# Attention stage: length rows as split products, the gate unit ahead of each step's scores, four output units in the last steps

## The chip, the cores and the metric

The kernel runs on one core of one Trainium2 chip, as one launch. The metric is the device time of that launch in microseconds (us), median of the runs. The engines are TensorE (PE in the rows, its weight loads PEld), VectorE (DVE), ScalarE (ACT), GpSimd (POOL) and SyncE (SP), which issues the weight loads of the kernel from DRAM. Each engine works through its own list of instructions; semaphores tie the lists together.

## The reference, cut to what matters

The model is two blocks of two layers each on 256 tokens of width 1024. The first block's layer is a feed-forward part, a token mixer and a second feed-forward part. The token mixer has a gated delta rule branch (y_a) and an attention branch (y_b):

```python
def mla(...):
    q = (rms_norm(q_lat, q_lat_gain) @ w_q_up).reshape(B, S, MLA_HEADS, MLA_QK)
    kv = (rms_norm(kv_lat, kv_lat_gain) @ w_kv_up).reshape(B, S, MLA_HEADS, QK_NOPE + V_HEAD)
    ...
    q = rms_norm(q, q_norm)
    k = rms_norm(k, k_norm)
    ...
    o = causal_block_attention(q, k, v)

def token_mix(...):
    y_a = gated_deltanet(...) @ w_branch_a
    y_b = mla(...) @ w_branch_b
    y = jax.nn.sigmoid(gate_a) * y_a + jax.nn.sigmoid(gate_b) * y_b
    return y @ w_out
```

gated_deltanet ends with an rms_norm of each head's output, times a gate. The change touches only the two token mixers of the first block (two layers).

## The kernel before

Everything lies transposed: 128 channels on the partitions, T = 256 tokens along the free axis, so a 1024-wide activation is 8 tiles of 128 x 256. All large products are float32 made of three rounded products (three_pass, L589 to L591): weights and activations are each split into a rounded part (hi) and the rest (lo), and hi x hi, lo x hi and hi x lo are added in PSUM. A **unit** is 128 x 1024 weights, 24 such matmuls of 128 x 256. SP streams the units in the order of use into a ring of 8 slots (raw), a slot being free once the unit 8 before it is done (unit_done). ScalarE rounds a unit to w_hi (split_hi, L544), VectorE subtracts to get w_lo (split_lo, L557; lo_ready), both 4 units ahead of TensorE (AHEAD).

Stages follow each other with their instructions written out by hand for each engine. In each of the two layers three stages matter here:

- **up** (up_tensor and so on): queries, keys and values from the latents. In between, the delta rule's heads get their lengths: o_sums adds squares, o_inverse and a Sqrt give rinv (16 rows, one per head), o_length (L1609) spreads row h over 128 partitions by a product of a column of the identity with rinv, in float32 with 16 rows. At its end the first two gate units (gate_a, m = 0, 1) run; the length rows of the attention heads (rinv16, named soft in the rows) are made from up_summed by a reciprocal and a Sqrt (L1782); L1755 turns them to columns.
- **attn** (attn_tensor and so on): 8 heads, one per step i. TensorE: length row of head i+2 (L1855), scores of head i (L1873, L1874; float32), gate unit i+2 (while i+2 < 8), then the turn of the weights of head i-3 (L1885, three transposes) and the product of head i-4 (L1893, L1894). VectorE: mask and maximum (L1922), nmx (L1926), keys of head i+2 (L1905, L1906), split_lo, the scaling of head i-1. ScalarE: Exp of head i (L1953), split_hi, the Tanh of gate unit i+1 (gate_a_scalar, L1846), the copy of the turned weights (pt, L1964) and of the product (qn, L1968). After step 5 there are no gate units left, and steps 6 to 11 hold scores, turns and products alone.
- **gates** (gates_tensor and so on): 24 units, gate_b (g), the output product of the delta rule branch (a) and of the attention branch (b), in the order GATE_UNITS; first both branch outputs are rounded and subtracted (o_hi L2014, o_lo L2042; 2048 columns each), then 8 units of w_out.

PSUM has 8 banks. The gate units use GATE_A_BANKS = (0, 1, 5, 7, 5, 7, 5, 7), so from m = 4 on a unit waits until the Tanh of unit m-2 has read its bank:

```python
    if m >= 4:
        pe.wait_ge(p.sem["gate_act"], attn.at("gate_act") + m - 1)
```

len_parts and pick_r are in use before the change too, in the projection stage: 64 rows of rounded parts and 64 of rests, of which pick_r takes one of each, so one rounded product of 128 rows spreads a length row (L1028).

Of the kernel before, what the change touches and what calls it, by code (L numbers as in the profile page):

```python
# [13 lines left out]
P = 128  # L14
T = 256
# [268 lines left out]
def signals(st):  # L284
# [15 lines left out]
    if kind == "gdn":  # L300
        n = dict(gdn_step=2 * PAIRS, cols_ready=1, exp_cum=1, rows_done=8,
                 kb_ready=8, exponent_ready=16, row_exp=8, decay_ready=8, pairs_done=8, pairs_used=16, sq_done=8,
                 inv_grown=2 * GROWN, turned_done=8, turned_used=8, first_turned=2 * PAIRS, conv_pad=1,
                 first_both=4 * PAIRS, lp_done=2 * MERGES, lq_done=2 * MERGES, new_ready=2 * MERGES, wu_done=8,
                 v0_ready=8, state_done=8, state_ready=8, v1_done=8, v1_ready=8, o_done=8,
                 out_ready=8, sums_done=1, inv_step=1, o_inv=1, o_sq=8, o_root=1, len_row=8, o_gated=8, oa_ready=8)
    if kind == "up":
        n = dict(lat_sq=6, up_out=20, up_summed=20, up_sq=20, lat_sum=1, lat_ready=5, lat_var=2,
                 lat_root=1, lat_rows=2, lat_scaled=5, lat_rounded=5, rope_in=5, rope_out=5, rope_step=10, rope_turned=5,
                 rinv_rows=1, values_out=4, head_var=3, cols_done=1, cols_ready=2)  # L310
    if kind == "attn":
# [41 lines left out]
class Program:  # L353


    def __init__(self, nc, ctx, stages, dram):
# [68 lines left out]
        self.qn = self.over("qn", 39936, [P, HEADS, T])  # L425
        self.qr = self.over("qr", 48128, [P, HEADS // 2, T])
        self.vt = self.over("vt", 52224, [P, 2, D])
        self.krz = self.over("krz", 60416, [P, HEADS, T])
        self.kr = self.over("kr", 68608, [P, T])
        self.work = self.over("work", 69632, [P, 2, T])  # L430
        self.rinv16 = self.soft
        self.sm = self.over("sm", 8192, [P, ATTN_AHEAD + 1, 3 * P])
        self.o_lo = self.over("o_lo", 8192, [P, 16, T], F32R)
        self.o_hi = self.over("o_hi", 48128, [P, 16, T], F32R)
# [1325 lines left out]
def up_scalar(p, act, st):  # L1760
    a, u0, nc, f = st.at, st.unit0, p.nc, p.nc.scalar.activation
    for j in range(N_UP):
        if j < 12:
            if j % 2 == 0:
                split_hi(p, act, u0 + AHEAD + j // 2)
            if j == 4:
                act.wait_ge(p.sem["o_inv"], st.gdn.at("o_inv") + 1)
                f(p.rinv[0:16], p.rinv[0:16], ACT.Sqrt).then_inc(p.sem["o_root"], 1)
        elif j % 4 == 0:
            split_hi(p, act, u0 + AHEAD + 6 + (j - 12) // 4)  # L1770
            act.wait_ge(p.sem["o_gated"], st.gdn.at("o_gated") + HEADS)
# [10 lines left out]
    f(p.rinv16[0:16], p.rinv16[0:16], ACT.Sqrt).then_inc(p.sem["rinv_rows"], 1)  # L1782


def up_vector(p, dve, st):
# [18 lines left out]
    for j in range(5):  # L1804
        out = p.kr[:] if j == 4 else p.qr[:, j]
# [5 lines left out]
    for s in range(8, 10):  # L1811
        split_lo(p, dve, u0 + AHEAD + s)

    dve.wait_ge(p.sem["up_summed"], a("up_summed") + N_UP)
    v.tensor_scalar(p.rinv16[0:16], p.psum[0:16, 6, 0:T], 1.0 / 192, EPS, ALU.mult, ALU.add).then_inc(
        p.sem["head_var"], 1)
    dve.wait_ge(p.sem["head_var"], a("head_var") + 2)
    v.reciprocal(p.rinv16[0:16], p.rinv16[0:16]).then_inc(p.sem["head_var"], 1)
# [29 lines left out]

def attn_tensor(p, pe, st):
# [3 lines left out]
    def length(h):  # L1853

        mm(p.psum[:, 2 + h % 2, 0:T], p.c("ident")[0:16, HEADS + h : HEADS + h + 1].to_broadcast([16, P]),  # L1855
           p.rinv16[0:16], start=True, stop=True).then_inc(p.sem["head_rinv"], 1)

    pe.wait_ge(p.sem["values_out"], a("values_out"))
    for h in range(2):
        length(h)  # L1860
    for i in range(HEADS + ATTN_AHEAD + 1):
        if i < HEADS:
# [13 lines left out]
        if i + 2 < KD:  # L1876
            gate_a(p, pe, st, i + 2)
# [20 lines left out]
def attn_vector(p, dve, st):  # L1898
# [15 lines left out]
    for i in range(HEADS + 1):  # L1914
# [16 lines left out]
        if i:  # L1931
# [7 lines left out]
                p.sem["weighed"], 1)  # L1939


def attn_scalar(p, act, st):
# [4 lines left out]
    for i in range(HEADS + ATTN_AHEAD + 1):  # L1947
        if i < HEADS:
# [29 lines left out]
def gates_tensor(p, pe, st):  # L1978
    a, u0 = st.at, st.unit0
    pe.wait_ge(p.sem["ob_out"], a("ob_out"))  # L1980
    freed = []
    for n, (kind, m) in enumerate(GATE_UNITS):
        if n >= 4:
            sem, count = freed[n - 4]
            pe.wait_ge(p.sem[sem], count)
        freed.append(("gate_act", a("gate_act") + m + 1) if kind == "g" else ("y_step", a("y_step") + 2 * m + (1 if kind == "a" else 2)))
        pe.wait_ge(p.sem["lo_ready"], u0 + n + 1)
        if kind != "g" and m == 0:
            pe.wait_ge(p.sem["o_split"], a("o_split") + (1 if kind == "a" else 2))
        hi, lo, first = dict(g=(p.h_hi, p.h_lo, 0), a=(p.o_hi, p.o_lo, 0), b=(p.o_hi, p.o_lo, 8))[kind]  # L1990
        for k in range(UNIT):
            ins = three_pass(p, p.psum[:, n % 4, 0:T], (u0 + n) % SLOTS, k, hi[:, first + k], lo[:, first + k],
# [15 lines left out]
def gates_scalar(p, act, st):  # L2008
# [28 lines left out]
def gates_vector(p, dve, st):  # L2037
    a, u0, v, x = st.at, st.unit0, p.nc.vector, st.x(p)
    for b, src in enumerate((p.qkv[:, 0:HEADS], p.qn[:])):
        dve.wait_ge(p.sem["o_rounded"], a("o_rounded") + b + 1)  # L2040
        part = slice(8 * b, 8 * b + 8)
        v.tensor_tensor(p.o_lo[:, part], src, p.o_hi[:, part].bitcast(F32), ALU.subtract).then_inc(p.sem["o_split"], 1)  # L2042
# [694 lines left out]
def plan():  # L2737
# [47 lines left out]
    for at, st in enumerate(stages):  # L2785
# [131 lines left out]
```

## Time and profile before

| | us |
|---|---|
| median of 3 runs | 3016.95 (3011.16 to 3019.12) |
| the profiled execution's own time | 3017.49 |
| its span in the profile | 3015.7 |
| TensorE busy | 2863.1 (95%) |
| VectorE busy | 2266.2 (75%) |
| ScalarE busy | 1405.8 (47%) |

The granted clock of TensorE is given in the window views as PEclk, where 1.00 is 2.4 GHz and 0.50 is 1.2 GHz; over the run its mean is 0.973. The attention stage of the first layer lies at 502 to 555 us, that of the second at 1301 to 1354. In the timeline a row's second number is the time from its start to its modelled end, and matmuls overlap, so the time that a piece of work takes on TensorE is read from start to start.

### The profile page before, as it was taken

Reading aid. Unit: us, or ns where it says so; the run is one execution under the profiler, and the core shown is the slowest. Engines: PE = TensorE matmul, PEld = TensorE weight load, DVE = VectorE, ACT = ScalarE, POOL = GpSimd, SP = SyncE. Lnnn points to the kernel's source line nnn. Section 1 sums busy time; section 2 is a strip of 40 time slices with the busy share of each in tenths; the row PEclk is TensorE's granted clock in tenths of the full one; section 3 lists DMA queues with packets and bytes.
Section 4 is the critical chain, followed back from the end, with each engine's and each line's share of the span. In section 5 each row is a group of like instructions: output and inputs, shape, how many; then the busy total and the mean of one; then the engine's idle time right before and its main releaser. Section 6 shows DMA issues by size and latency. Waiting matters only on the chain.

```text
span 3015.7 us, 61676 instructions
## 1 busy us (share of the span) xinstructions
PE 2863.1 (95%) x24692; PEld 2753.7 (91%) x24692; DVE 2266.2 (75%) x3616; ACT 1405.8 (47%) x2286; POOL 414.9 (14%) x444
## 2 busy tenths in 40 slices
PE   5999999999999999999999999899999999998998
PEld 5999887899999988779999999799987999998998
DVE  7999665578877786556787888788887688777554
ACT  3436533444444464444444446544676444443342
POOL 0025001010200210200102012201036101002001
PEclk9999999999999999999999999999999899999899
DMA  8995302358967642125787885388421488675353
GB/s 339 355 367 181 126 9 99 132 190 332 333 232 281 220 166 71 57 71 189 255 309 265 309 322 170 122 316 324 169 99 64 164 310 328 226 264 187 119 188 127
DMA packets 172726, 632.21 MB, mean 210 GB/s; under 512 B 19168, under 2 KB 19552, under 8 KB 172000
## 3 DMA queue, kind: packets, MB, share of 16 engines
q1 hardware_dynamic: 123696, 450.79, 41.6%
q10 hardware_dynamic: 48816, 178.41, 16.6%
q8 instruction: 154, 2.52, 0.3%
q14 instruction: 60, 0.49, 0.1%
HBM read 628.07 MB, written 1.05 MB: 209 GB/s over the span
## 4 chain that ended last, share of the span: by engine, by line
PE 86%; DVE 9%; ACT 3%; issue 1%; DMA 1%; POOL 0%; DVEq 0%; ACTq 0%; POOLq 0%
PE psum L589 24%; PE psum L590 23%; PE psum L591 23%; DVE w_lo L557 3%; PE psum L607 1%; PE psum L608 1%; DVE ada_w L636 1%; DVE xl L2315 1%; PE psum L613 1%; PE psum L2411 1%; PE psum L1523 1%; PE psum L1526 1%; ACT w_hi L544 1%; PE psum L2431 1%; PE psum L2425 1%
## 5 line engine op out<-in xcount | busy, mean ns | idle before, releaser
L589 PE MATMUL psum<-h_hi,w_hi 128*128 128x256 f32 x4464 | 1256.3, 281 | 0.9 <-ACT qn L1968 0.9
L590 PE MATMUL psum<-h_hi,w_lo 128*128 128x256 f32 x4464 | 1250.6, 280 | 0.0
L591 PE MATMUL psum<-h_lo,w_hi 128*128 128x256 f32 x4464 | 1248.5, 280 | 0.0
L557 DVE TENSOR_TENSOR w_lo<-raw,w_hi 128x1024 fp32r<-128x1024 f32 x852 | 1065.9, 1253 | 180.1 <-ACT w_hi L544 179.2
L544 ACT ACTIVATE w_hi<-raw 128x1024 fp32r<-128x1024 f32 x852 | 875.6, 1055 | 386.9 <-DMA raw<-stream_dram 232.8
L589 PEld LDWEIGHTS psum<-h_hi,w_hi 128*128 128x128 f32 x4464 | 843.0, 189 | 3.7 <-ACT qn L1968 1.3
L590 PEld LDWEIGHTS psum<-h_hi,w_lo 128*128 128x128 f32 x4464 | 842.9, 189 | 0.7 <-issue 0.2
L591 PEld LDWEIGHTS psum<-h_lo,w_hi 128*128 128x128 f32 x4464 | 842.7, 189 | 0.0
L590 PE MATMUL psum<-u_hi,w_lo 128*128 128x256 f32 x1584 | 442.7, 279 | 0.0
L589 PE MATMUL psum<-u_hi,w_hi 128*128 128x256 f32 x1584 | 442.5, 279 | 0.0
L591 PE MATMUL psum<-u_lo,w_hi 128*128 128x256 f32 x1584 | 441.9, 279 | 0.0
L636 DVE CUSTOM_DVE_ANT_0 ada_w<-ada_w,tmp 128x1024 f32<-128x1024 f32 x312 | 386.0, 1250 | 3.4 <-ACT tmp L644 3.4
L901 ACT ACTIVATE gate<-psum 128x256 f32<-128x256 f32 x198 | 76.1, 384 | 587.1 <-PE psum L591 573.6
L730 POOL TENSOR_TENSOR tmp<-x 128x256 f32<-128x256 f32 x91 | 112.3, 1237 | 1629.7 <-DVE x L951 1235.0
L591 PEld LDWEIGHTS psum<-u_lo,w_hi 128*128 128x128 f32 x1584 | 297.8, 188 | 0.0
L590 PEld LDWEIGHTS psum<-u_hi,w_lo 128*128 128x128 f32 x1584 | 297.7, 188 | 0.0
L589 PEld LDWEIGHTS psum<-u_hi,w_hi 128*128 128x128 f32 x1584 | 297.7, 188 | 0.0
L928 DVE TENSOR_TENSOR mid<-gate,psum 128x256 f32<-128x256 f32 x198 | 83.5, 422 | 206.2 <-ACT gate L901 206.1
L607 PE MATMUL psum<-h_hi,w_hi 128*128 128x256 f32 x208 | 77.3, 383 | 21.1 <-ACT h_hi L795 21.1
L1136 DVE SCALAR_TENSOR_TENSOR qkv<-conv_in,par,qkv 128x256 f32<-128x256 f32 x144 | 81.5, 567 | 12.6 <-ACT conv_in L1055 9.2
L734 POOL TENSOR_TENSOR tmp<-tmp 128x256 f32<-128x256 f32 x78 | 89.4, 1147 | 6.1
L936 DVE TENSOR_TENSOR u_lo<-mid,u_hi 128x256 fp32r<-128x256 f32 x198 | 84.2, 425 | 6.9
(397 smaller groups left out, 3409.0 us busy)
## 6 DMA issues: line engine op xcount, KB each, us to landing
raw<-stream_dram SPq DMA_DIRECT2D x852, 512.0 KB, 4.3
ada_w<-ada_dram ACTq DMA_DIRECT2D x328, 512.0 KB, 4.9
tmp<-c_dram ACTq DMA_DIRECT2D x8, 512.0 KB, 3.5
x<-x_dram SPq DMA_DIRECT2D x1, 1024.0 KB, 10.1
ctx_x<-ctx_dram ACTq DMA_DIRECT2D x1, 1024.0 KB, 4.9
means<-means_dram ACTq DMA_DIRECT2D x1, 1024.0 KB, 4.9
out_dram<-tmp SPq DMA_DIRECT2D x1, 1024.0 KB, 3.9
const<-const_dram SPq DMA_DIRECT2D x1, 753.0 KB, 13.4
```

Source lines behind the costliest of these rows:

```text
L544: p.nc.scalar.activation(p.w_hi[:, slot].rearrange("p k m -> p (k m)"), p.raw[:, slot], ACT.Copy).then_inc(p.sem["hi_ready"], 1)
L557: p.nc.vector.tensor_tensor(p.w_lo[:, slot].rearrange("p k m -> p (k m)"), p.raw[:, slot], p.w_hi[:, slot].rearrange("p k m -> p (k m)").b ...
L589: mm(out, p.w_hi[:, slot, k], hi, start=start, stop=False, skip_group_check=skip)
L590: mm(out, p.w_lo[:, slot, k], hi, start=False, stop=False, skip_group_check=skip)
L591: return mm(out, p.w_hi[:, slot, k], lo, start=False, stop=stop, skip_group_check=skip)
L607: mm(out, p.w_hi[:, slot, k], p.h_hi[:, k], start=start, stop=False, skip_group_check=True)
L636: p.nc.vector.tensor_tensor_reduce(p.ada_w[:, slot], p.ada_w[:, slot], row, 1.0, 0.0, ALU.mult, ALU.add, p.ada_raw[:, s : s + 1]).then_inc ...
L730: p.nc.gpsimd.tensor_tensor(to, x[:, m], x[:, m], mult).then_inc(p.sem["sq_ready"], 1)
L734: p.nc.gpsimd.tensor_tensor(p.sq_sum, p.sq_sum, to, ALU.add).then_inc(p.sem["sq_ready"], 1)
L928: nc.vector.tensor_tensor(p.mid[:, t % 2], p.gate[:, t % 2], p.psum[:, t % 2, T : 2 * T], ALU.mult).then_inc(p.sem["mid_step"], 1)
L936: nc.vector.tensor_tensor(p.u_lo[:, t], p.mid[:, t % 2], p.u_hi[:, t].bitcast(F32), ALU.subtract).then_inc(p.sem["mid_ready"], 1)
L1136: nc.vector.scalar_tensor_tensor(out, src[:, j : j + T], w[:, t, j : j + 1], out, ALU.mult, ALU.add).then_inc(p.sem["conv_step" if j < 2 e ...
```

## The change

Three edits, in both layers.

1. **Length rows as split products.** o_length and length(h) use pick_r and len_parts with 128 rows, one rounded product each. ScalarE copies the root's rounded part to rows 0 to 15 of len_parts, VectorE puts the rest in rows 64 to 79. In up_vector the attention heads' reciprocal goes ahead of the last rotation (j = 4).
2. **The gate unit first in each step.** gate_a(i + 2) stands ahead of the length row and the scores of step i, not behind them. Its waits are as they were.
3. **Four a units in the last steps.** GATE_UNITS begins with a0 to a3; early_a runs them in steps 7 to 10. The rounding of the delta rule branch (oa_hi, oa_lo) is done in four pieces of 512 columns in steps 0 to 3, ahead of the Tanh on ScalarE. The a units have PSUM banks 2, 3, 0, 1, and their first step on VectorE (early_y) and three splits go to the end of the attention stage. The SBUF places of some tiles move.

```diff
-GATE_UNITS = [("g", 0), ("g", 1)]
+EARLY_A = 4
+GATE_UNITS = [("a", _m) for _m in range(EARLY_A)] + [("g", 0), ("g", 1)]
 for _m in range(KD):
-    GATE_UNITS += [("a", _m), ("b", _m)] + ([("g", _m + 2)] if _m + 2 < KD else [])
+    GATE_UNITS += [("a", _m)] * (_m >= EARLY_A) + [("b", _m)] + ([("g", _m + 2)] if _m + 2 < KD else [])
...
 def o_length(p, pe, gdn, h):
     if h == 0:
-        pe.wait_ge(p.sem["o_root"], gdn.at("o_root") + 1)
+        pe.wait_ge(p.sem["inv_step"], gdn.at("inv_step") + 2)
...
-        p.psum[:, 4 + h % 2, 0:T], p.c("ident")[0:16, h : h + 1].to_broadcast([16, P]), p.rinv[0:16], start=True, stop=True
+        p.psum[:, 4 + h % 2, 0:T], p.pick_r[:, h : h + 1].to_broadcast([P, P]), p.len_parts[:], start=True, stop=True
...
                 f(p.rinv[0:16], p.rinv[0:16], ACT.Sqrt).then_inc(p.sem["o_root"], 1)
+                act.wait_ge(p.sem["o_root"], st.gdn.at("o_root") + 1)
+                f(p.len_parts[0:16], p.rinv[0:16], ACT.Copy).then_inc(p.sem["o_root"], 1)
...
+        if s == 1:
+            dve.wait_ge(p.sem["o_root"], st.gdn.at("o_root") + 2)
+            v.tensor_tensor(
+                p.len_parts[ROWS : ROWS + 16], p.rinv[0:16], p.len_parts[0:16].bitcast(F32), ALU.subtract
+            ).then_inc(p.sem["inv_step"], 1)
...
+def early_a(p, pe, gates, n):
+
+    s = gates.unit0 + n
+    if n == 0:
+        pe.wait_ge(p.sem["o_split"], gates.at("o_split"))
+    pe.wait_ge(p.sem["lo_ready"], s + 1)
+    for k in range(UNIT):
+        ins = three_pass(p, p.psum[:, OUT_BANKS[n], 0:T], s % SLOTS, k, p.oa_hi[:, k], p.oa_lo[:, k], k == 0, k == UNIT - 1)
+    ins.then_inc(p.sem["unit_done"], 1)
...
     for i in range(HEADS + ATTN_AHEAD + 1):
+        if i + 2 < KD:
+            gate_a(p, pe, st, i + 2)
+        if i == HEADS - 1:
+            pe.wait_ge(p.sem["head_normed"], a("head_normed") + HEADS)
+            early_a(p, pe, st.gates, 0)
+        if i == HEADS:
+            early_a(p, pe, st.gates, 1)
+        if i == HEADS + 1:
+            pe.wait_ge(p.sem["masked"], a("masked") + HEADS)
+            early_a(p, pe, st.gates, 2)
+        if i == HEADS + 2:
+            early_a(p, pe, st.gates, 3)
         if i < HEADS:
...
-        if i + 2 < KD:
-            gate_a(p, pe, st, i + 2)
...
             split_hi(p, act, st.unit0 + AHEAD + i)
+        if i < 4:
+            pair = slice(2 * i, 2 * i + 2)
+            if i == 0:
+                act.wait_ge(p.sem["oa_ready"], a("oa_ready"))
+            f(p.oa_hi[:, pair], p.qkv[:, pair], ACT.Copy).then_inc(p.sem["o_rounded"], 1)
         if 1 <= i < KD - 1:
             gate_a_scalar(p, act, st, i + 1)
...
 def gates_tensor(p, pe, st):
     a, u0 = st.at, st.unit0
-    pe.wait_ge(p.sem["ob_out"], a("ob_out"))
```

TensorE, first layer, steps 1 and 2 of the attention stage: the scores of head 1 (kn, krz), then the next unit (h_hi, w_hi; 24 matmuls, the first shown). Before:

```order
L1873 MATMUL psum<-kn,qn 128x128 [waits gate_act]
L1874 MATMUL psum<-krz,qr 128x128
L1873 MATMUL psum<-kn,qn 128x256
L1874 MATMUL psum<-krz,qr 128x256
L589 MATMUL psum<-h_hi,w_hi 128x256 [waits lo_ready]
...
L1855 MATMUL psum<-soft,const 128x256 [waits head_normed]
L1873 MATMUL psum<-kn,qn 128x128 [waits masked]
L1874 MATMUL psum<-krz,qr 128x128
L1873 MATMUL psum<-kn,qn 128x256
L1874 MATMUL psum<-krz,qr 128x256
L589 MATMUL psum<-h_hi,w_hi 128x256 [waits gate_act,lo_ready]
```

After:

```order
L1930 MATMUL psum<-kn,qn 128x128 [waits gate_act]
L1931 MATMUL psum<-krz,qr 128x128
L1930 MATMUL psum<-kn,qn 128x256
L1931 MATMUL psum<-krz,qr 128x256
L598 MATMUL psum<-h_hi,w_hi 128x256 [waits gate_act,lo_ready]
...
L1899 MATMUL psum<-len_parts,pick_r 128x256 [waits head_normed]
L1930 MATMUL psum<-kn,qn 128x128 [waits masked]
L1931 MATMUL psum<-krz,qr 128x128
```

The first unit with a wait for gate_act (unit 4, which needs the Tanh of unit 2) stood behind the scores of head 2 and now stands directly behind those of head 1.

ScalarE, the same layer, steps 1 and 2. sm is a head's scores and weights, tmp the gate. Before:

```order
L1953 ACTIVATE sm,den<-sm,nmx,cols 128x128 [waits max_ready]
L1953 ACTIVATE sm,den<-sm,nmx,cols 128x256
L544 ACTIVATE w_hi<-raw 128x1024 [waits raw_full_0]
L1846 ACTIVATE tmp<-psum 128x256 [waits unit_done]
L1953 ACTIVATE sm,den<-sm,nmx,cols 128x128 [waits max_ready]
```

After:

```order
L2017 ACTIVATE sm,den<-sm,nmx,cols 128x128 [waits max_ready]
L2017 ACTIVATE sm,den<-sm,nmx,cols 128x256
L553 ACTIVATE w_hi<-raw 128x1024 [waits raw_full_0]
L2025 ACTIVATE oa_hi<-qkv 128x512
L1868 ACTIVATE tmp<-psum 128x256 [waits unit_done]
L2017 ACTIVATE sm,den<-sm,nmx,cols 128x128 [waits max_ready]
```

The Tanh keeps its place behind the Exp of the same step and has a rounding more ahead of it.

TensorE at the end of the attention stage, from the turn of head 7's weights on. Before:

```order
L1885 MATMUL psum<-const,sm 128x128 [waits weights_out,weighed]
L1885 MATMUL psum<-const,sm 128x128 x2
L1893 MATMUL psum<-pt,vt 128x256 [waits ob_out,weights_out]
L1894 MATMUL psum<-pt,vt 128x128
L1893 MATMUL psum<-pt,vt 128x256 [waits ob_out,weights_out]
L1894 MATMUL psum<-pt,vt 128x128
L589 MATMUL psum<-h_hi,w_hi 128x256 [waits lo_ready,ob_out]
```

After, from the third a unit on (the first of its 24 matmuls shown):

```order
L598 MATMUL psum<-oa_hi,w_hi 128x256 [waits lo_ready,masked]
...
L1940 MATMUL psum<-const,sm 128x128 [waits weights_out,weighed]
L1940 MATMUL psum<-const,sm 128x128 x2
L1948 MATMUL psum<-pt,vt 128x256 [waits ob_out,weights_out]
L1949 MATMUL psum<-pt,vt 128x128
L598 MATMUL psum<-oa_hi,w_hi 128x256 [waits lo_ready]
```

A unit of the output product now stands ahead of each of the last groups of turn and product, and the first gate unit of the next stage has no wait for ob_out.

## Rows read from the trace of the kernel before

**Rows 1.** The page: busy time by engine, and the chain that ended last.

```profile
PE 2863.1 (95%) x24692; PEld 2753.7 (91%) x24692; DVE 2266.2 (75%) x3616; ACT 1405.8 (47%) x2286; POOL 414.9 (14%) x444
...
PE 86%; DVE 9%; ACT 3%; issue 1%; DMA 1%; POOL 0%; DVEq 0%; ACTq 0%; POOLq 0%
```

**Rows 2.** Waits of TensorE, 440 to 620 us: total, times, longest.

```profile
PE psum L1885 <- ACT pt L1964: 4.9, 2, 3.4
```

**Rows 3.** Timeline of TensorE (start, duration): length rows, rounded and float32.

```profile
336.19 0.52 PE L1028 MATMUL psum<-len_parts,pick_r 128*128 128x256 f32 x3
336.54 0.28 PE L589 MATMUL psum<-h_hi,w_hi 128*128 128x256 f32 x1
...
457.57 1.12 PE L1609 MATMUL psum<-rinv,const 16*128 16x256 f32 x4
458.63 0.38 PE L589 MATMUL psum<-lat_hi,w_hi 128*128 128x256 f32 x1
```

**Rows 4.** Timeline of TensorE, start of the attention stage, waits in brackets.

```profile
502.51 0.61 PE L1755 MATMUL psum<-const,soft 16*128 16x16 f32 x4 [0.53 <-ACT soft L1782]
...
504.71 0.69 PE L1855 MATMUL psum<-soft,const 16*128 16x256 f32 x2 [0.63 <-DVE krz L1906]
```

**Rows 5.** Timeline of TensorE: scores 1, unit, row, scores 2; scores 5.

```profile
512.85 0.59 PE L1874 MATMUL psum<-krz,qr 128*128 128x256 f32 x2
513.09 0.47 PE L589 MATMUL psum<-h_hi,w_hi 128*128 128x256 f32 x1
...
516.18 0.69 PE L1855 MATMUL psum<-soft,const 16*128 16x256 f32 x2
516.80 0.49 PE L1873 MATMUL psum<-kn,qn 128*128 128x128 f32 x2
...
517.78 0.59 PE L1874 MATMUL psum<-krz,qr 128*128 128x256 f32 x2
...
533.90 0.59 PE L1874 MATMUL psum<-krz,qr 128*128 128x256 f32 x2
```

**Rows 6.** Timeline of VectorE and ScalarE behind scores 1.

```profile
513.48 0.29 DVE L1922 CUSTOM_DVE_ANT_0 sm<-psum,const 128x128 f32<-128x128 f32 x1 [1.52 <-PE psum L1874]
...
514.36 0.49 ACT L1953 ACTIVATE sm<-sm,nmx,cols 128x128 f32<-128x128 f32 x1 [3.65 <-DVE nmx L1926]
...
515.43 1.04 ACT L544 ACTIVATE w_hi<-raw 128x1024 fp32r<-128x1024 f32 x1
516.38 0.36 ACT L1846 ACTIVATE tmp<-psum 128x256 f32<-128x256 f32 x1
```

**Rows 7.** Timeline of ScalarE at the end of the attention stage.

```profile
554.54 0.38 ACT L1968 ACTIVATE qn<-psum 128x256 f32<-128x256 f32 x1 [1.07 <-PE psum L1894]
554.96 1.91 ACT L2014 ACTIVATE o_hi<-qkv 128x2048 fp32r<-128x2048 f32 x1
```

**Rows 8.** Timeline of TensorE, last steps of the attention stage.

```profile
539.44 0.49 PE L1885 MATMUL psum<-const,sm 128*128 128x128 f32 x3
...
540.42 0.28 PE L1873 MATMUL psum<-kn,qn 128*128 128x128 f32 x1
...
547.96 0.87 PE L1885 MATMUL psum<-const,sm 128*128 128x128 f32 x3 [3.38 <-ACT pt L1964]
...
554.98 0.38 PE L589 MATMUL psum<-h_hi,w_hi 128*128 128x256 f32 x1 [0.47 <-ACT qn L1968]
```

**Rows 9.** TensorE after it stood; windows: length, busy by engine, PEclk, DMA share.

```profile
330.43 1.24 PE L1028 MATMUL psum<-len_parts,pick_r 128*128 128x256 f32 x3 [3.78 <-DVE qkv L1169]
...
1874.70 0.72 PE L2118 MATMUL psum<-const,xl 128*128 128x128 f32 x4 [2.33 <-ACT b_tok L2199]
...
330.40:335.80 5.40, 5.37 (x24) 5.28 (x25) 4.89 (x12) 0.00 (x0) 0.00 (x0) 0.51 0.00 0
1875.08:1878.60 3.52, 3.52 (x20) 3.52 (x19) 3.41 (x7) 2.95 (x7) 0.00 (x0) 0.52 0.04 14
...
543.40:547.20 3.80, 1.17 (x7) 0.94 (x7) 1.82 (x9) 2.01 (x6) 0.00 (x0) 1.00 0.00 0
```

More of the change, by code:

```diff
@@ L205, in first_mix_units, with y_steps @@
     return out
-GATE_UNITS = [("g", 0), ("g", 1)]
+EARLY_A = 4
+GATE_UNITS = [("a", _m) for _m in range(EARLY_A)] + [("g", 0), ("g", 1)]
 for _m in range(KD):
-    GATE_UNITS += [("a", _m), ("b", _m)] + ([("g", _m + 2)] if _m + 2 < KD else [])
+    GATE_UNITS += [("a", _m)] * (_m >= EARLY_A) + [("b", _m)] + ([("g", _m + 2)] if _m + 2 < KD else [])
+def y_steps(kind, m):
+    done = [unit for unit in GATE_UNITS if unit[0] != "g"]
+    return done.index((kind, m)) + 1
 def ssd_in_units(w_in, context):
@@ L424, in __init__ @@
         self.kn = self.over("kn", 24576, [P, HEADS, T])
[L425 to L430, printed above, removed]
+        self.qn = self.over("qn", 40960, [P, HEADS, T])
+        self.qr = self.over("qr", 49152, [P, HEADS // 2, T])
+        self.vt = self.over("vt", 53248, [P, 2, D])
+        self.krz = self.over("krz", 61440, [P, HEADS, T])
+        self.kr = self.over("kr", 69632, [P, T])
+        self.work = self.over("work", 70656, [P, 2, T])
         self.rinv16 = self.soft
         self.sm = self.over("sm", 8192, [P, ATTN_AHEAD + 1, 3 * P])
[L433 to L434 removed]
+        self.oa_lo = self.over("oa_lo", 0, [P, HEADS, T], F32R)
+        self.oa_hi = self.over("oa_hi", 32768, [P, HEADS, T], F32R)
+        self.ob_lo = self.over("ob_lo", 16384, [P, HEADS, T], F32R)
+        self.ob_hi = self.over("ob_hi", 56320, [P, HEADS, T], F32R)
         self.y = self.over("y", 24576, [P, KD, T])
@@ L1810, in up_vector @@
         v.tensor_tensor(out, out, p.work[:, j % 2], ALU.add).then_inc(p.sem["rope_out"], 1)
[L1811 to L1818, printed above, removed]
+    split_lo(p, dve, u0 + AHEAD + 8)
+    dve.wait_ge(p.sem["rinv_rows"], a("rinv_rows") + 2)
+    v.tensor_tensor(
+        p.len_parts[ROWS : ROWS + 16], p.rinv16[0:16], p.len_parts[0:16].bitcast(F32), ALU.subtract
+    ).then_inc(p.sem["head_var"], 1)
+    split_lo(p, dve, u0 + AHEAD + 9)
     cols = p.psum[:, 6, T : T + 2 * 2 * HEADS].rearrange("p (c b h) -> p c b h", c=2, b=2)[:, :, 0]
@@ L1939, in attn_vector @@
                 p.sem["weighed"], 1)
+        if i < 4:
+            pair = slice(2 * i, 2 * i + 2)
+            dve.wait_ge(p.sem["o_rounded"], a("o_rounded") + i + 1)
+            v.tensor_tensor(p.oa_lo[:, pair], p.qkv[:, pair], p.oa_hi[:, pair].bitcast(F32), ALU.subtract).then_inc(
+                p.sem["o_split"], 1)
+    for n in range(EARLY_A):
+        if n < 3:
+            split_lo(p, dve, st.gates.unit0 + AHEAD + n)
+        early_y(p, dve, st.gates, n)
 def attn_scalar(p, act, st):
@@ L1979, in gates_tensor @@
     a, u0 = st.at, st.unit0
-    pe.wait_ge(p.sem["ob_out"], a("ob_out"))
     freed = []
     for n, (kind, m) in enumerate(GATE_UNITS):
[L1983 to L1986, printed above, removed]
+        freed.append(("gate_act", a("gate_act") + m + 1) if kind == "g" else ("y_step", a("y_step") + y_steps(kind, m)))
+        if n < EARLY_A:
+            continue
+        sem, count = freed[n - 4]
+        pe.wait_ge(p.sem[sem], count)
         pe.wait_ge(p.sem["lo_ready"], u0 + n + 1)
-        if kind != "g" and m == 0:
-            pe.wait_ge(p.sem["o_split"], a("o_split") + (1 if kind == "a" else 2))
-        hi, lo, first = dict(g=(p.h_hi, p.h_lo, 0), a=(p.o_hi, p.o_lo, 0), b=(p.o_hi, p.o_lo, 8))[kind]
+        if (kind, m) == ("b", 0):
+            pe.wait_ge(p.sem["o_split"], a("o_split") + 1)
+        hi, lo = dict(g=(p.h_hi, p.h_lo), a=(p.oa_hi, p.oa_lo), b=(p.ob_hi, p.ob_lo))[kind]
         for k in range(UNIT):
-            ins = three_pass(p, p.psum[:, n % 4, 0:T], (u0 + n) % SLOTS, k, hi[:, first + k], lo[:, first + k],
+            ins = three_pass(p, p.psum[:, OUT_BANKS[n % 4], 0:T], (u0 + n) % SLOTS, k, hi[:, k], lo[:, k],
                              k == 0, k == UNIT - 1)
@@ L2025, in gates_scalar @@
             if m >= 2:
-                act.wait_ge(p.sem["y_step"], a("y_step") + 2 * m - 2)
-            f(p.gate_t[:, m % 2], p.psum[:, n % 4, 0:T], ACT.Tanh, scale=0.5).then_inc(p.sem["gate_act"], 1)
+                act.wait_ge(p.sem["y_step"], a("y_step") + y_steps("b", m - 2))
+            f(p.gate_t[:, m % 2], p.psum[:, OUT_BANKS[n % 4], 0:T], ACT.Tanh, scale=0.5).then_inc(p.sem["gate_act"], 1)
         if n == LAST_GATE:
@@ L2051, in gates_vector @@
     for n, (kind, m) in enumerate(GATE_UNITS):
-        split_lo(p, dve, u0 + AHEAD + n)
-        if kind == "a":
+        if n >= 3:
+            split_lo(p, dve, u0 + AHEAD + n)
+        if kind == "a" and n >= EARLY_A:
             dve.wait_ge(p.sem["unit_done"], u0 + n + 1)
             v.scalar_tensor_tensor(
-                p.y[:, m], p.tmp[:, m], 1.0, p.psum[:, n % 4, 0:T], ALU.add, ALU.mult
+                p.y[:, m], p.tmp[:, m], 1.0, p.psum[:, OUT_BANKS[n % 4], 0:T], ALU.add, ALU.mult
             ).then_inc(p.sem["y_step"], 1)
```

49 lines of the change are left out of this document (33 added, 16 removed).

## Prediction

> **What bounds the kernel now.** Read the page first: TensorE is busy 95% of the span and is 86% of the chain that ended last [rows 1]. So a microsecond counts if TensorE issues less, waits less or runs at a higher clock. Next come its waits from 440 to 620 us, the first attention stage with its neighbours: the longest, 4.9 us in two pieces, is for the copy of turned weights on ScalarE [rows 2]. The second layer (1250 to 1460 us) shows the same waits within 0.1 us, so everything below is per layer and counts twice. Then TensorE's timeline gives the length of each step of the attention stage [rows 4, 5, 8], and those of VectorE and ScalarE what follows a step's scores [rows 6]. The reader should see that the middle steps have no wait now, and why: a gate unit lies between a step's scores and the next unit that needs the other engines to be done.
>
> All times are from the one profiled execution: span 3015.7 us, time 3017.49, which is 0.5 above the median 3016.95 of the runs. The sum is made on 3017.5.
>
> **Length rows.** Two groups of eight rows change from a float32 product to one rounded product. A pair in the up stage holds TensorE from 457.57 to 458.63, 1.06 us; three rounded rows in the projection stage hold it from 336.19 to 336.54, 0.12 each [rows 3]. Four pairs: 4 x (1.06 - 0.24) = **3.3 us** less, and TensorE has no wait there that could take it back. The copy and the subtraction that are added (16 x 256 each) are about 0.4 us by the Tanh of 256 columns with 0.36 [rows 6], on engines that wait for TensorE in that stage: nothing on the path. If that cover were gone they would cost 0.8. For the attention rows the root's chain now starts ahead of the last rotation and ends under two gate units of 5.6 us, so the wait of 0.53 [rows 4] goes. The other eight rows are in the steps below.
>
> **Head: to the end of scores 1.** The last unit ahead of it ends at 501.98 (502.51 less its wait, rows 4), scores 1 end at 512.85 + 0.59 = 513.44 [rows 5]: 11.5 us with one gate unit in it. After: columns 0.5, changes of type 0.4, two rows 0.2, then twice unit 2.8 (24 matmuls at 0.117), row 0.12, change 0.2, scores 1.57, less 0.3 where the first scores' end overlaps the next unit: 10.2 us with two gate units. The keys of the first head, which made the wait of 0.63 [rows 4], are under the unit. **1.3 us** less, and one unit fewer is left for later.
>
> **Steps 2 to 5: the wait that the order lays open.** Gate unit i+2 writes the PSUM bank of unit i, so it waits for the Tanh of unit i (gate_act). ScalarE runs that Tanh in step i-1, behind the Exp of head i-1, and that Exp waits for scores i-1. Before, a whole unit (about 3 us), a row and the scores of head i stand between scores i-1 and unit i+2. After, the unit stands right behind scores i-1 (or behind one group of turned weights and product). The chain from the end of scores 1 at 513.44: mask from 513.48, Exp from 514.36, weight split from 515.43, Tanh 516.38 to 516.74 [rows 5, 6], 3.30 us. In steps 0 to 3 ScalarE now also rounds 512 columns ahead of the Tanh: a quarter of the 2048-column rounding of 1.91 [rows 7] is 0.48, half of the 1024-column split of 1.04 [rows 6] is 0.52; I take 0.5. From ScalarE's end to TensorE's first matmul is 554.92 to 554.98 = 0.06 [rows 7, 8]. So scores to unit is 3.86 in steps 2, 3 and 4 and 3.36 in step 5. From the unit's first matmul to the end of its scores now takes 513.09 to 518.37 = 5.28; the row falls from 516.18 to 516.80 = 0.62 to 0.12 [rows 5], and 4.76 is left. Together 3 x 8.62 + 8.12 = 34.0 us. Before, scores 1 to scores 5 took 513.44 to 534.49 = 21.05 [rows 5]. **12.9 us more.** Behind the waiting unit on TensorE stand the row and the scores of the next head; VectorE's mask, ScalarE's Exp and the next Tanh wait for those, so each step pays again. The first and last bound: nothing, if the Tanh comes first (rival A); 4.4 instead of 3.86 if the rounding and semaphores cost double.
>
> The Trainium skill (TensorE: Matmul & The Clock Gate, Architectural detail) says that ScalarE and VectorE take their queues strictly in order and that TensorE pulls only weight loads ahead, no matmul. By that the wait stands whole; were the Tanh free to run as soon as its unit is done, the time would be rival A's. The trace is with the page: TensorE stood 3.38 us for a copy of turned weights (547.96, rows 8) that stands behind an Exp and a split in ScalarE's list.
>
> **Tail: end of scores 5 to the first gate unit of the next stage.** Before 534.49 to 554.98 = 20.5 us, with gate unit 7 in it. A group (three turns, one product) takes 539.44 to 540.42 = 0.98 [rows 8]; the groups late in the tail stand on waits of 4.9 us in all [rows 2] and on a lower clock (three turns 0.87 at 547.96, 0.49 at 539.44, rows 8). After, by the same durations: group 1.0, scores 6 1.5, a wait of 1.4 (the copy of turned head 2 is behind Exp 5, split and Tanh 6, 3.9 us behind scores 5), group 1.0, unit 2.9, scores 7 1.6, group 1.0, unit 2.9, wait 0.2, group 1.0, unit 2.9, group 1.0, unit 2.9, group 1.0, wait 0.8 (the last product still waits for the copy of head 6), product 0.6: 23.7 us with four units of the output product. **3.2 us** more here, and 4 x 2.8 = **11.2 us** fewer in the next stage: the waits are filled as the order means it. The 2048-column rounding of 1.91 [rows 7] and its subtraction on VectorE, not longer than 2.5 by its size, begin after the last copy and are under two gate units of 5.6; uncovered they would cost under 1 us. The weight loads on SP's queue come in the new order of use, and the DMA share is 0.04 or less in the quiet pieces of rows 9, so no load is late.
>
> **Sum at full clock, per layer:** -3.3 - 1.3 + 12.9 + 3.2 - 11.2 = **+0.3 us**. The new wait eats the gain.
>
> **Clock.** TensorE stood 2.33 us until 1874.70, and then ran 3.5 us at a granted clock of 0.52; it stood 3.78 us until 330.43 and ran 5.4 us at 0.51; after the shorter of the two waits of rows 2 (4.9 less 3.4, 1.5 us) it stayed at 1.00 up to 547.20 [rows 9]. 0.5 is 1.2 GHz of 2.4. In 3.5 us at 0.5 half the work is done, so the four waits (3.9, 3.9, 3.5 and 2.4 us free of work, since groups fill 0.3 and 1.0 of the last two) cost 1.7 to 2.7 us each. I take 2.0, nearer to the shorter stretch, for which there are more cases. **+8.0 us per layer.** The old losses of this kind are not in the new sums, which use durations at full clock.
>
> Total: 2 x (0.3 + 8.0) = 16.6; 3017.5 + 16.6 = 3034, less 0.5 for the median, rounded down: **3033 us**, 0.5% slower.
>
> **Rivals.** A, on the other side: the wait for gate_act is hidden. Its place is the first matmul of gate units 4 to 7. Its price is all four waits (3.9 + 3.9 + 3.5 + 2.4 = 13.7), the 1.4 in the tail and the clock's 8.0: 23.1 less per layer, 3033 - 46 = **2987 us**. It decides when the Tanh is done within the 0 to 1.0 us of work that is left between scores and unit. Against it: the 3.30 us of rows 5 and 6, on two engines in order; for it: only that unit and scores lie side by side without a wait today. B: the waits come but the clock stays high, as it did up to 547.20: 3017 + 2 x 0.3 = **3017 us**. Against it: a stand of 2.33 us was enough at 1874.70. C: the clock stays low through whole steps 2 to 5 and a unit behind: a unit then loses 24 x 0.1 = 2.4, its scores about 1.2, so 4 x 3.6 + 2.4 = 16.8 per layer, 3017 + 2 x 17.1 = **3051 us**. For it: 5.4 us at 0.51 [rows 9] is longer than a step's 4.8 us of work.
>
> **Chances.** Forecast 0.59, A 0.11, B 0.14, C 0.16. The forecast's own range is +0.3 +/- 2 and a clock of 6 to 11 per layer: 3025 to 3043. The 8-in-10 range takes in B and most of the way to C: 3015 to 3047. A measurement of this kernel tells about 0.3% (9 us) from no change. Slower by more (over 3026): 0.50 of the forecast's 0.59 and C, 0.66; within: the rest of the forecast and B, 0.23; faster: A, 0.11.
>
> **What the changed profile would show.** Four waits of TensorE per layer at the first matmul of a gate unit, released by the Tanh on ScalarE, near 3.9, 3.9, 3.5 and 2.4 us; no wait for keys or root; length rows of 0.12 us; in the tail one wait of about 1.4 and one under 1; a granted clock near 0.8 from scores 1 to scores 5. If those waits are missing or under 1 us, the forecast is wrong and A is right; if they are there and the clock is 1.0, B; if it is 0.5 to 0.65 throughout, C.

## The result, and the profile after

| | us |
|---|---|
| changed kernel, median of 13 runs | 3023.66 (3019.67 to 3027.25) |
| kernel before, median of 13 runs | 3017.3 (3011.16 to 3024.86) |
| ratio | 1.0022 (95% interval 1.0014 to 1.0029) |
| the changed kernel's span in the profile | 3022.1 |

The change makes the kernel 0.2% slower. 3033 was forecast: the sign is right, the size is not; 16 us were forecast and 6.4 came. The measured time lies inside the range (3015 to 3047), and the difference is within the 0.3% that counted as no change, to which the text gave 0.23. Each experiment below has 4 runs (6 for the Tanh between Exp and split, 10 for the fillers, 5 for each of the last two), and its ratio is to runs of the kernel before that were timed alongside. One run of edit 1 alone took 4673.33 us at a mean granted clock of 0.557, where its others have 0.974 to 0.977, and is left out of the median and the ratio given for it.

TensorE's waits around the first attention stage (total, times, longest):

```profile
PE psum L598 <- ACT tmp L1868: 14.6, 4, 4.5
PE psum L1940 <- ACT pt L2033: 1.8, 2, 1.5
PE psum L1948 <- ACT qn L2037: 0.6, 1, 0.6
```

L598 is the first product of a gate unit, L1868 the Tanh. The 4.9 us for turned weights [rows 2] fell to 1.8, and four waits for the Tanh of 14.6 us in all came. Both layers have the same row. The first of them and its unit in TensorE's timeline (start, duration, wait):

```profile
505.67 0.59 PE L1931 MATMUL psum<-krz,qr 128*128 128x256 f32 x2
...
510.82 0.36 PE L598 MATMUL psum<-h_hi,w_hi 128*128 128x256 f32 x1 [4.55 <-ACT tmp L1868]
...
515.24 0.28 PE L1899 MATMUL psum<-len_parts,pick_r 128*128 128x256 f32 x1
```

Scores 1 end at 506.26, the unit starts at 510.82 and takes 4.42 us until the length row, where it took 3.09 before with the change of type in it [rows 5]. The row is one record now. The windows of TensorE (length, busy time of PE, PEld, DVE, ACT, POOL, then PEclk, DMA share, GB/s) give the clock of the unit behind the first, the third and the fourth wait:

```profile
510.82:515.24 4.42, 4.42 (x24) 4.42 (x25) 1.55 (x5) 0.00 (x0) 0.00 (x0) 0.61 0.00 0
...
530.78:535.21 4.43, 4.43 (x24) 4.43 (x25) 1.55 (x5) 0.23 (x1) 0.00 (x0) 0.61 0.02 4
540.25:543.15 2.90, 2.90 (x25) 2.90 (x25) 1.47 (x4) 0.50 (x2) 0.00 (x0) 1.00 0.00 0
```

The unit behind the fourth wait (2.46 us) ran at the full clock. In the second layer the waits are the same, and the unit behind the first of them ran wholly at half clock:

```profile
1314.49:1319.75 5.26, 5.26 (x24) 5.26 (x25) 1.56 (x5) 0.00 (x0) 0.00 (x0) 0.50 0.01 3
```

To compare kernels I use one region per layer: from the latents' rows (L1591) to the first product of the next norm, with the up, attention and gates stages in it. Everything that the change touches is inside. The windows of the two regions in the kernel before, same columns:

```profile
441.45:645.07 203.62, 196.07 (x1415) 172.85 (x1415) 120.46 (x223) 93.02 (x166) 28.80 (x33) 0.98 0.37 127
1240.10:1443.80 203.70, 196.11 (x1415) 172.91 (x1415) 120.49 (x224) 92.90 (x166) 28.77 (x33) 0.98 0.37 127
```

And in the changed kernel:

```profile
439.55:647.49 207.94, 190.75 (x1398) 172.08 (x1398) 121.16 (x228) 93.97 (x171) 28.00 (x33) 0.98 0.38 125
1243.26:1452.83 209.57, 192.39 (x1398) 173.72 (x1398) 121.12 (x228) 94.07 (x171) 28.03 (x33) 0.96 0.37 123
```

The regions are 4.3 and 5.9 us longer, 10.2 together. TensorE is busy 5 us less in the first and stands longer. The rest of the program, where both kernels have the same instructions, took 3.8 us less in this profile; together that gives the 6.4 of the spans.

### The profile page after: what moved, and what is told of

Read it like the earlier page. It is cut to its first block, busy times and chain, and to the rows that moved or that the text cites. A ratio compares the mean times of both kernels' runs of the same rounds, so it can differ in the third digit from the quotient of the medians.

```text
span 3022.1 us, 61632 instructions
## 1 busy us (share of the span) xinstructions
PE 2848.6 (94%) x24660; PEld 2745.9 (91%) x24660; DVE 2267.4 (75%) x3626; ACT 1408.2 (47%) x2296; POOL 415.4 (14%) x444
## 4 chain that ended last, share of the span: by engine, by line
PE 84%; DVE 9%; ACT 4%; issue 1%; DMA 1%; POOL 0%; ACTq 0%; DVEq 0%; POOLq 0%
PE psum L598 23%; PE psum L600 23%; PE psum L599 23%; DVE w_lo L566 3%; PE psum L616 1%; PE psum L617 1%; DVE ada_w L645 1%; ACT w_hi L553 1%; DVE xl L2384 1%; PE psum L622 1%; PE psum L1532 1%; PE psum L2480 1%; PE psum L1535 1%; PE psum L2500 1%; PE psum L2494 1%
## 5 line engine op out<-in xcount | busy, mean ns | idle before, releaser
L598 PE MATMUL psum<-h_hi,w_hi 128*128 128x256 f32 x4464 | 1256.8, 282 | 29.2 <-ACT tmp L1868 29.2
L598 PEld LDWEIGHTS psum<-h_hi,w_hi 128*128 128x128 f32 x4464 | 846.3, 190 | 33.4 <-issue 32.5
L598 PE MATMUL psum<-u_hi,w_hi 128*128 128x256 f32 x1584 | 441.7, 279 | 0.0
L598 PEld LDWEIGHTS psum<-u_hi,w_hi 128*128 128x128 f32 x1584 | 297.7, 188 | 0.0
```

What stands on the lines that cost most here:

```text
L598: mm(out, p.w_hi[:, slot, k], hi, start=start, stop=False, skip_group_check=skip)
```

## The experiments

The theory is that of the prediction: the change gains what it means to gain, and the unit ahead of the scores opens a wait for the Tanh, which costs itself and some clock. The regions of the two layers are given as "first / second", from the same window view.

**Edit 1 alone.** The kernel before with o_length, length, up_scalar and up_vector of the changed one (only the length rows of the attention stage are shown here):

```diff
-        mm(p.psum[:, 2 + h % 2, 0:T], p.c("ident")[0:16, HEADS + h : HEADS + h + 1].to_broadcast([16, P]),
-           p.rinv16[0:16], start=True, stop=True).then_inc(p.sem["head_rinv"], 1)
+        mm(p.psum[:, 2 + h % 2, 0:T], p.pick_r[:, HEADS + h : HEADS + h + 1].to_broadcast([P, P]),
+           p.len_parts[:], start=True, stop=True).then_inc(p.sem["head_rinv"], 1)
```

> The kernel before with edit 1 alone (length rows as rounded products, root chain ahead of the last rotation). Theory: TensorE is the bound and has no wait in steps 0 to 5, so all 16 rows per layer count: 3.1 us in the up stage (as the changed kernel showed) and 0.5 for each of the rows of the attention stage plus the 0.53 wait for the root, together about 6.5 per layer, 13 in all: 3004. Rival: the rows of the attention stage only hand their time to waits in the tail, where ScalarE's copies end last: 6 to 7 us in all, 3011.

Measured: 3000.57 us, ratio 0.9924 (0.9904 to 0.9944). The window of the first region:

```profile
439.71:635.14 195.43, 187.77 (x1399) 168.62 (x1399) 120.63 (x225) 93.73 (x168) 27.99 (x33) 0.98 0.40 133
```

The second is 195.54. That is 8.2 less per layer, more than either side expected. The rows give what the theory said (columns 3.9 us earlier, root wait included; from scores 1 to scores 5 18.6 us instead of 21.1), but the head had something that I had left out: from scores 0 to scores 1 takes 4.2 us from start to start instead of 6.5. Before, this stretch ran partly at half clock. (From scores 5 to the end of the region this kernel is 1.2 us slower, 112.3 instead of 111.2: the waits for turned weights are 5.4 instead of 4.9, and more of the work there falls at half clock.) The window of the kernel before over it:

```profile
506.00:512.00 6.00, 6.00 (x32) 5.31 (x31) 2.82 (x8) 2.12 (x5) 0.00 (x0) 0.72 0.02 4
```

And the window of this kernel over the same place:

```profile
503.00:508.00 5.00, 5.00 (x42) 4.90 (x41) 2.80 (x9) 2.95 (x7) 0.00 (x0) 1.00 0.30 105
```

This kernel still waits for the keys, and 1.0 us instead of 0.63; so the keys' wait by itself doesn't explain the fall. The root wait and six records of float32 length rows stood ahead of it too, and which of them decides stays open.

**Edit 2 alone.** The kernel before with the two lines moved:

```diff
     for i in range(HEADS + ATTN_AHEAD + 1):
+        if i + 2 < KD:
+            gate_a(p, pe, st, i + 2)
         if i < HEADS:
...
-        if i + 2 < KD:
-            gate_a(p, pe, st, i + 2)
```

> The kernel before with edit 2 alone (gate unit ahead of the scores). Theory: the wait for gate_act comes without the rounding, 4 waits near 3.4 us (less what the groups fill), each of the longer ones followed by a gate unit at half clock (4.4 instead of 2.85 us), and nothing fills the tail: about 16 us per layer more, 3049. Rival: the waits need edit 3's rounding on ScalarE and are under 1 us without it: within 5 us of 3017.

Measured: 3059.14 us, ratio 1.0126 (1.0110 to 1.0143). TensorE's waits in the first layer (total, times, longest):

```profile
PE psum L589 <- ACT tmp L1846: 12.4, 4, 3.4
PE psum L1885 <- ACT pt L1964: 6.2, 3, 2.4
```

The longest wait is 3.4 us, as read from rows 5 and 6, without any rounding ahead of the Tanh: the rival falls. The regions are 225.55 / 223.53, 22 and 20 us longer, above the 16 expected. TensorE stands 13 and 14 us longer: the 12.4 for the Tanh, and waits for the copies of turned weights that are added in the tail (4.9 becomes 6.2 and 7.2). It is also busy 9.0 and 5.7 us longer, for the same work at a lower clock. In the first layer the clock fell in or behind all four waits, the last of 2.46 us too, and again in the tail, as the windows show:

```profile
549.33:553.47 4.14, 4.14 (x25) 3.92 (x25) 1.47 (x4) 0.51 (x2) 0.00 (x0) 0.68 0.00 0
564.50:574.70 10.20, 7.63 (x26) 6.17 (x27) 4.45 (x16) 5.27 (x14) 0.00 (x0) 0.50 0.00 0
```

**The changed kernel with edit 2 undone.**

> The changed kernel with edit 2 undone (gate unit behind the scores again), edits 1 and 3 kept. Theory: the 14.6 us of waits per layer, the 1.5 in the tail and the half clock (4.7 us) go, the head gets 1 to 2 us longer: 16 to 18 us per layer less than 3023.7, about 2990. Rival: the rounding in ScalarE and the output units are themselves a cost in the middle or the tail, and the time stays above 3005.

Measured: 2986.52 us, ratio 0.9891 (0.9873 to 0.9909). TensorE's waits in the first layer (total, times, longest); all for the Tanh but 1.9 us are gone:

```profile
PE psum L598 <- ACT tmp L1868: 1.9, 3, 1.0
PE psum L1899 <- DVE krz L1961: 1.0, 1, 1.0
PE psum L1948 <- ACT qn L2037: 0.6, 1, 0.6
```

The window of this kernel's first region:

```profile
440.49:629.40 188.91, 185.23 (x1398) 166.87 (x1398) 120.73 (x228) 93.96 (x171) 27.90 (x33) 1.00 0.41 137
```

So edit 2 costs 19.0 / 20.6 us of region. In the first layer, edits 1 and 3 together gain 14.7, and edit 3 adds 6.5 to edit 1. Edit 3 does what it is for: no wait for turned weights is left in this kernel. The mean clock of the region is 1.00.

**The changed kernel with the Tanh ahead of the Exp.**

```diff
     for i in range(HEADS + ATTN_AHEAD + 1):
+        if 1 <= i < KD - 1:
+            gate_a_scalar(p, act, st, i + 1)
         if i < HEADS:
...
-        if 1 <= i < KD - 1:
-            gate_a_scalar(p, act, st, i + 1)
```

> The changed kernel with the Tanh of gate unit i+1 moved ahead of the Exp of head i on ScalarE, nothing else. Theory: the Tanh is then done before TensorE comes to unit i+3, so the waits of 14.6 us per layer go with the clock's share: 20 us per layer less, 2983, and the head's gain stays, so it is faster than the kernel with the unit behind the scores. Rival: VectorE, whose step is 5.5 us (mask, keys, split, scaling, subtraction) against 4.6 of TensorE in steps 0 to 2, becomes the bound and makes waits of about 1 us each for the keys or the mask: 2990 or above.

Measured: 2988.93 us, ratio 0.9901 (0.9885 to 0.9918). The order of edit 2 is kept, only ScalarE's is changed. TensorE's waits in the first layer, none of them for the Tanh:

```profile
PE psum L1940 <- ACT pt L2033: 2.7, 2, 2.0
PE psum L598 <- DVE w_lo L566: 1.0, 3, 0.6
PE psum L1948 <- ACT qn L2037: 0.6, 1, 0.6
```

This shows that the waits come from the Tanh's place in ScalarE's list. The regions are 191.24 / 191.26, 16.7 and 18.3 less than the changed kernel's, where 20 was expected, and the kernel is not faster than the one with the unit behind the scores, as the theory had it. The rest is partly the rival, three waits on VectorE for split weights with 1.0 us; partly the wait for turned weights in step 6, 2.0 us where it was 1.5 (with the last gate unit in step 5 ahead of the scores, steps 5 and 6 have nothing behind them); and partly the clock, which fell behind that wait in both layers. The turn, the product and the unit behind it take 5.41 us:

```profile
533.53:538.94 5.41, 5.41 (x31) 5.22 (x32) 3.15 (x10) 3.15 (x9) 0.00 (x0) 0.68 0.00 0
```

**The Tanh between Exp and split.**

```diff
             ins.then_inc(p.sem["exped"], 1)
+            if 1 <= i < KD - 1:
+                gate_a_scalar(p, act, st, i + 1)
             split_hi(p, act, st.unit0 + AHEAD + i)
```

> The changed kernel with the Tanh between the Exp and the weight split on ScalarE, so that the split (0.95) and, in steps 0 to 3, the rounding (0.52) no longer stand ahead of it. Theory: the waits fall from 4.55, 3.96, 3.63, 2.46 to about 3.1, 2.5, 2.1 and 1.5, and since the wait of 2.46 was followed by a unit at full clock, the clock falls after one of the four at most: 5.4 us of waits and 3 of clock per layer less, 3007. Rival: the clock falls after every wait over 2 us as it does now, and only the waits shrink: 3013.

Measured: 3008.89 us, ratio 0.9965 (0.9947 to 0.9983). The four waits of the first layer are 3.08, 2.49, 2.16 and 1.51; the first two in TensorE's timeline:

```profile
510.49 0.36 PE L598 MATMUL psum<-h_hi,w_hi 128*128 128x256 f32 x1 [3.08 <-ACT tmp L1868]
...
517.45 0.36 PE L598 MATMUL psum<-h_hi,w_hi 128*128 128x256 f32 x1 [2.49 <-ACT tmp L1868]
```

The regions are 197.70 / 199.25. In the first layer the clock did not fall at all, as the window behind the first wait shows (PEclk is the third column from the end):

```profile
511.00:516.00 5.00, 3.96 (x31) 3.50 (x29) 3.42 (x11) 0.94 (x3) 0.00 (x0) 1.00 0.26 78
```

The second layer's region is 1.55 longer with the same waits. There the clock fell behind the first of them, and the unit took 4.42 us instead of 2.88:

```profile
1304.12:1308.54 4.42, 4.42 (x24) 4.42 (x25) 2.45 (x5) 1.32 (x2) 0.00 (x0) 0.61 0.01 4
```

So the theory's 3007 holds and the rival, a fall after every wait over 2 us, falls: of the six such waits of both layers one brought the clock down. The same 3.08 us of standing did in one layer and did not in the other.

**Filler matmuls in the waits.**

```diff
+FILL = (34, 30, 27, 16)
...
+        if 2 <= i < KD - 2:
+            pe.wait_ge(p.sem["masked"], a("masked") + i - 1)
+            for _ in range(FILL[i - 2]):
+                mm(p.psum[:, i % 2, 3 * P : 4 * P], p.h_hi[:, 0, 0:P], p.h_hi[:, 0, P:T], start=True, stop=True)
         if i + 2 < KD:
             gate_a(p, pe, st, i + 2)
```

> The changed kernel with rounded 128-column matmuls of no use (34, 30, 27, 16 of them, into columns of PSUM that nobody reads) ahead of the four waiting gate units, so that TensorE works while it would wait. Theory: the half clock behind the first three waits comes from the wait, so the units take 2.85 instead of 4.42 us: about 5 us per layer less, 3013. Rival: the units are slow for another reason (the change between float32 and rounded products, PSUM, SBUF) or the fillers outlast the waits: 3024 or above.

Measured: 3016.54 us, ratio 0.9993 (0.9982 to 1.0005). Against the changed kernel's 1.0022 that is some 9 us less; the medians, taken at different times, differ by 7. The fillers and the wait that is left, in TensorE's timeline:

```profile
508.98 4.09 PE L1911 MATMUL psum<-h_hi 128*128 128x128 f32 x34
513.88 0.36 PE L598 MATMUL psum<-h_hi,w_hi 128*128 128x256 f32 x1 [0.81 <-ACT tmp L1868]
```

And the windows of the unit behind, in the first and in the second layer:

```profile
513.88:516.85 2.97, 2.97 (x25) 2.97 (x26) 1.55 (x5) 0.00 (x0) 0.00 (x0) 1.00 0.00 0
...
1309.27:1313.70 4.43, 4.43 (x24) 4.43 (x25) 1.55 (x5) 0.00 (x0) 0.00 (x0) 0.61 0.01 4
```

From the start of the last record of scores 1 to the unit it is 5.15 us in this kernel as in the changed one, so the fillers do nothing but keep TensorE at work. In the first layer the units behind the waits then run at 1.00 and the region is 5.4 us less than the changed kernel's (202.58): this is the price of the clock there. In the second layer the clock fell all the same behind the first fillers, with 0.81 us of standing, and the region (204.86) is 4.7 less. What the clock cost the changed kernel there is more than that, by the 1.5 us that this one unit still loses.

**Edits 1 and 3 with the Tanh first, without and with one unit ahead.** The kernel with edit 2 undone and the Tanh ahead of the Exp:

> Edits 1 and 3 with the gate unit behind the scores, and the Tanh of gate unit i+1 ahead of the Exp of head i. Theory: what was left of the waits for the Tanh with the unit behind the scores (1.9 us per layer in three pieces, for the rounding that stands ahead of it) goes: about 4 us less than with the Tanh in its place, 2983. Rival: VectorE's step, 5.5 us against 4.3 of TensorE, makes up for it with waits for the split weights or the turned weights, and the time is the same 2987 or, as with the unit ahead and the Tanh first, 2989.

Measured: 2986.9 us, ratio 0.9891 (0.9872 to 0.9911); regions 188.88 / 188.92, the same as with the Tanh in its place. The 1.9 us of waits for the Tanh are gone and 2.4 for turned weights have come: the rival is right. TensorE's waits in the first layer:

```profile
PE psum L1940 <- ACT pt L2033: 2.4, 2, 1.9
PE psum L1899 <- DVE krz L1961: 1.0, 1, 1.0
PE psum L1948 <- ACT qn L2037: 0.6, 1, 0.6
```

Then with only gate unit 2 ahead of the first scores (gate_a(2) behind the first two length rows, and none behind scores 0):

> The same with one gate unit (2) ahead of the first scores and the others behind the scores of their step as before, so that step 0 has no unit behind its scores. Theory: the unit ahead covers the scaling of the first keys, which TensorE waited 1.0 us for with all units behind, and nothing is opened by it: 2 us less than the kernel with only the Tanh moved, 2981. Rival: with scores 0 and 1 side by side, scores 1 or 2 wait for mask or keys on VectorE and the microsecond comes back: no less, or up to 2 us more.

Measured: 2990.0 us, ratio 0.9904 (0.9885 to 0.9923); regions 191.28 / 191.26, 2.4 more: the rival is right here too. The wait for the keys is gone, and the wait for turned weights grew to 4.1 us, as TensorE's waits in the first layer show:

```profile
PE psum L1941 <- ACT pt L2034: 4.1, 2, 2.1
PE psum L1949 <- ACT qn L2038: 0.6, 1, 0.6
```

With the kernel that has all units ahead and the Tanh first (191.24) this says that edit 2 gains nothing even without its waits: against the same kernel with the units behind (188.88) it costs 2.4 us per layer. Only 0.3 of that is standing time (0.8 with one unit ahead); for the rest TensorE is busy longer. All three kernels wait for the same turn, of head 3 in step 6: 2.02 us with all units ahead, 2.03 with one, 1.89 with none. Behind the first two the clock fell, in both layers, and behind the third it did not. Its turn, product and unit take 3.81 us instead of 5.41:

```profile
531.85:535.66 3.81, 3.81 (x31) 3.76 (x32) 2.07 (x9) 2.02 (x7) 0.00 (x0) 1.00 0.00 0
```

So most of the 2.4 us is a fall of the clock, and the 0.1 us more of waiting does not explain it: the kernel with one unit ahead also stood 2.08 us for an earlier turn, and the clock stayed up behind that. That the later steps lack the unit that was moved to the front shows only in the standing time. Why the clock fell at the one turn and not at the others stays open.

## Why the prediction was wrong in size

The terms, for the first layer, read from start to start as in the prediction:

| term | forecast | measured | from |
|---|---|---|---|
| length rows of the up stage, and the root wait | -3.8 | -3.9 | columns at 61.1 us of the region, then 57.2 |
| columns to scores 1, a unit more | -0.8 | -1.4 | 10.9, then 9.5 |
| scores 1 to scores 5, at full clock | +12.9 | +12.8 | 21.05, then 38.47 less 4.6 |
| tail to the first gate unit | +3.2 | +2.7 | 20.49, then 23.17 |
| next stage, four units fewer | -11.2 | -10.5 | 90.09, then 79.59 |
| sum at full clock | +0.3 | -0.3 | |
| clock | +8.0 | +4.6 | three units of 4.42 instead of 2.90 |
| sum | +8.3 | +4.3 | region 203.62, then 207.94 |

- **The wait** is right, in its place, number and cause. 3.86, 3.86, 3.5 and 2.4 were forecast; 4.55, 3.96, 3.63 and 2.46 came. (The 4.76 of the working is 4.78 by its own rows, which changes nothing.) The rounding of 512 columns takes 0.61 (0.52 from start to start). The first wait is 0.7 longer, mostly since I took VectorE to be free: the mask of head 1 began at 506.90, 0.64 after the end of scores 1, because the split and the subtraction added in step 0 were still running until 506.99.
- **The tail** is right: 1.52 at the turn of head 3, where 1.4 was said, then 0.27 and 0.57.
- **The clock is the step that failed.** "I take 2.0" for each of four waits was mis-sized twice. The fourth wait cost nothing. Each of the other three cost 1.5 in the first layer (4.42 less 2.90), where the clock fell within the first matmuls of the unit and was back before the scores. In the second layer the same waits cost 6.1 us: in the first two the clock fell while TensorE still stood and stayed low through the unit, which took 5.26 and 5.10. That is 10.7 us for both layers in place of 16. The fillers put the price near that, at 5.4 in the first layer and at 4.7 and the 1.5 that was still lost in the second. With 10.7 the sum would have been 3028. The rows at hand (2.33, 3.78) were taken for a price per wait, when they only show that a stand of this size can bring the clock down. The sign given for the clock, near 0.8 from scores 1 to scores 5, was closer than its price: 0.87 and 0.79.
- **The head** was 0.6 better than said. For each of the two steps in it 0.12, 0.2 and 1.57 were put in for row, change of type and scores, 1.89 together; from the row to the end of the scores takes 1.59 (504.67 to 506.26). That the 11.5 us of before hold a piece at half clock, which edit 1 alone takes away, was not seen, but it was in the number that the sum began from.
- **What stays open.** The clock does not explain the whole miss. Of the forecast 16.6 us the regions show 10.2; 5.3 of the difference is the clock, 1.1 the other terms. The medians and the profiled spans show only +6.4. The prediction put the rest of the program, which has the same instructions, at no change, and it took 2608.4 before and 2604.6 after. In the profiles of the eight experiments it lies between 2604.3 and 2609.5 without an order that fits any edit. So single profiles carry some 5 us there, but 13 runs of each kernel should not; why the medians don't show the region's 10 us isn't settled. Each region is from one profile, and the clock's part in it differs by 1.5 us between the two layers of one run.

Rival A (the wait hidden) is refuted by the trace of the changed kernel. Its 2987 is nearly met by the kernel with the Tanh first, 2988.93, but this does not confirm the price of 23.1 per layer that was given with it: the regions say 16.7 and 18.3. The clock's 8.0 is in that price and in the 3033 that it was taken from, and cancels. So 2987 rests on the terms at full clock alone, and these were nearly right (+0.3 against -0.3 per layer). The 1.4 in the tail, which A also takes away, did not go; it became 2.0. B (waits, but full clock) holds for one wait in four. C did not come.

Edits 1 and 3 without edit 2 are the fastest version here, with the Tanh in its place or first: 2986.52 and 2986.9 us, 1.1% less than before.

## What to carry to other kernels

Before work is moved ahead on the bound engine, look up every semaphore that the moved work waits for, and ask which instruction of another engine raises it and what that one stands behind; here the first unit with such a wait came 1.3 us after its Tanh was done, and after the move four units stood for 2.5 to 4.5 us. If such an order is wanted, move the releasing instruction ahead in its own list too, and look at what the moved work leaves uncovered at the other end of the loop: here it left a wait of 2.0 us for turned weights in step 6, and the clock fell behind it. A gain of some microseconds from three edits at once should be timed edit by edit: by the ratios, two of these gained 1.1% and the third took 1.3%.

## What the runs showed of the hardware

- The granted clock after a stand is not a function of the stand's length alone. In the changed kernel it fell behind 3.63 us and more and not behind 2.46; with edit 2 alone it fell behind a stand of 2.46 too. With the Tanh in the middle it did not fall behind 3.08 in the first layer and did in the second. In waits for turned weights it fell behind 2.02 and 2.03 us in both layers of two kernels, but not behind 2.08 in one of these kernels nor behind 1.89 in a third. For a unit or turn behind a stand of 2 to 4.6 us the price was between 0 and 2.4 us (a unit of 2.90 against one of 5.26).
- Matmuls of no use in place of a wait kept the clock at 1.00 through the first layer's region, which became 5.4 us shorter. They are no guarantee: in the second layer the clock fell once, behind 4.09 us of them and 0.81 us of standing (unit of 4.43 us instead of 2.97).
- A float32 length row of 16 rows costs 0.5 us in a stream of rounded products and a rounded one of 128 rows 0.12. The sixteen rows of a layer and what hung on them (the root wait, the half clock in the head) were worth 8.2 us.
